# Last tiles' norm and stores rebuilt, step-size block in two products for three, and GpSimd's loads for the down sums begun behind their stores

## The reference

```python
h = rms_norm(x, norm_mix_pre)
proj = h @ w_in                      # q, k, v, z, xbc, and 32 columns of raw step sizes (dt_raw)
attn = neighbourhood_attention(q, k, v, rpb); attn = rms_norm(attn, attn_out_norm)
ssd = ssd_mixer(z, xbc, dt_raw, ...)  # dt = softplus(dt_raw + dt_bias), scans both ways
x = x + rms_norm(concat([attn, ssd]) @ w_out, norm_mix_post)
h = rms_norm(x, norm_ffn_pre)
gate = depthwise_conv(h @ w_gate, ffn_conv_w, ffn_conv_b)
f = (gelu(gate) * (h @ w_up)) @ w_down          # 2816 hidden channels
y = x + rms_norm(f, norm_ffn_post)
rms_norm(x, g) = x / sqrt(mean(x * x) + 1e-6) * g
```

## Time and profile before

| | |
|---|---|
| three runs | 2920.98 us median (2919.64 to 2925.11) |
| the profiled execution | 2929.13 us, span 2927.4 us |
| PE busy | 2810.8 us, 96% |
| DVE, ACT, POOL busy | 2036.0, 1279.8, 639.4 us |
| mean granted TensorE clock | 0.986 |

### The profile page before, as it was taken

One profiled execution on the slowest core, in us unless ns is written; L12 is line 12 of the kernel. 1 busy time (PEld: TensorE's weight loads), 2 busy tenths in 40 slices (PEclk: granted clock), 3 DMA queues, 4 the chain that ended last, 5 costly groups with the idle time before them and its releaser, 6 DMA issues.

```text
span 2927.4 us, 36565 instructions
## 1 busy us (share of the span) xinstructions
PE 2810.8 (96%) x12784; PEld 2227.4 (76%) x12784; DVE 2036.0 (70%) x3119; ACT 1279.8 (44%) x2547; POOL 639.4 (22%) x849
## 2 busy tenths in 40 slices
PE   7999999889999999999999999998999999999996
PEld 5878787568777778888778787875677788888885
DVE  3657754894788887775647577459857877777656
ACT  4224555345743223345533255552557333333443
POOL 4622222670014530000100322227500000000001
PEclk9999999989999999999999999999899999999998
DMA  7551232314535441253532422331246222114334
GB/s 224 140 146 55 67 102 90 113 31 157 182 130 194 166 165 51 69 175 115 193 102 69 130 61 73 120 119 51 80 140 197 77 80 78 67 58 155 97 115 140
DMA packets 150229, 334.84 MB, mean 114 GB/s; under 512 B 22353, under 2 KB 25073, under 8 KB 150048
## 3 DMA queue, kind: packets, MB, share of 16 engines
q1 hardware_dynamic: 112688, 202.54, 21.9%
q0 software_dynamic: 37360, 129.97, 13.3%
HBM read 264.51 MB, written 69.90 MB: 114 GB/s over the span
## 4 chain that ended last, share of the span: by engine, by line
PE 74%; DVE 15%; issue 4%; ACT 4%; DMA 2%; POOL 0%; SPq 0%; DVEq 0%; ACTq 0%; POOLq 0%
PE G L649 4%; PE G L651 4%; PE G L650 4%; PE A L1139 4%; PE A L1140 4%; PE A L1141 4%; PE A L1087 4%; PE A L1088 4%; PE A L1089 4%; PE G L1087 4%; PE G L1089 4%; PE G L1088 4%; PE G L679 3%; PE G L680 2%; PE G L681 2%
## 5 line engine op out<-in xcount | busy, mean ns | idle before, releaser
L1725 DVE TENSOR_TENSOR wlo<-raw,whi 128x512 fp32r<-128x512 f32 x630 | 437.4, 700 | 485.1 <-ACT whi L1212 482.6
L1212 ACT CAST whi<-raw 128x512 fp32r<-128x512 f32 x630 | 382.8, 619 | 447.2 <-PE A L1141 149.8
L649 PE MATMUL G<-arena_rounded,whi 128*128 128x512 f32 x800 | 330.6, 413 | 6.6 <-DVE wlo L1725 3.8
L651 PE MATMUL G<-arena_rounded,wlo 128*128 128x512 f32 x800 | 316.2, 395 | 0.0
L650 PE MATMUL G<-arena_rounded,whi 128*128 128x512 f32 x800 | 316.1, 395 | 0.0
L1087 PE MATMUL G<-arena_rounded,whi 128*128 128x512 f32 x560 | 222.3, 397 | 3.1 <-DVE wlo L1725 1.5
L1087 PE MATMUL A<-arena_rounded,whi 128*128 128x512 f32 x560 | 222.0, 396 | 2.7 <-DVE small L2315 1.6
L1089 PE MATMUL G<-arena_rounded,wlo 128*128 128x512 f32 x560 | 221.5, 396 | 0.0
L1089 PE MATMUL A<-arena_rounded,wlo 128*128 128x512 f32 x560 | 221.5, 396 | 0.0
L1088 PE MATMUL G<-arena_rounded,whi 128*128 128x512 f32 x560 | 221.5, 395 | 0.0
L1088 PE MATMUL A<-arena_rounded,whi 128*128 128x512 f32 x560 | 221.4, 395 | 0.0
(11 more groups left out here) (345 smaller groups left out, 6222.4 us busy)
## 6 DMA issues: line engine op xcount, KB each, us to landing
raw<-w_gu_tiles SPq DMA_DIRECT2D x184, 256.0 KB, 3.3
raw<-w_out_rows SPq DMA_DIRECT2D x144, 256.0 KB, 2.9
raw<-w_tok_tiles SPq DMA_DIRECT2D x96, 256.0 KB, 2.7
raw<-w_in_tiles SPq DMA_DIRECT2D x92, 256.0 KB, 2.9
raw<-sums_of_down SPq DMA_DIRECT2D x88, 256.0 KB, 2.7
raw<-w_down_rows SPq DMA_DIRECT2D x66, 256.0 KB, 2.8
f_by_chunk<-small POOLq DMA_DIRECT2D x24, 512.0 KB, 4.6
arena<-w_down_rows POOLq DMA_DIRECT2D x22, 512.0 KB, 7.2
```

What stands on the lines that cost most here:

```text
L649: nc.tensor.matmul(out, whi[:, u % SPLIT_SLOTS, w], hi, start=first, stop=False)
L651: return nc.tensor.matmul(out, wlo[:, u % SPLIT_SLOTS, w], hi, start=False, stop=last)
L1212: nc.scalar.copy(whi[:, u % SPLIT_SLOTS, w], weights_of(u)).then_inc(S["hi_split"], 1)
L1725: tt(wlo[:, u % SPLIT_SLOTS, w], weights_of(u), whi[:, u % SPLIT_SLOTS, w].bitcast(F), ALU.subtract).then_inc(S["lo_split"], 1)
```

## The change

Four things are edited.

1. The step-size block. DVE writes the low part of the 32 real columns into the zero columns 32 to 63 of `whi`, so that two products for three (`gemm_dt`) give high and low halves in different partitions of the same bank. ACT copies partitions 32 to 63 out, and DVE adds them. `tail_stats` and `tail_out` of the previous sequence's last four tiles move one input block ahead, to blocks 1 and 2.
2. GpSimd's loads for the down sums: those of block p are issued right behind the stores of sums p - 1, before the wait for the next f.
3. The last four tiles. In sequence 1 SP loads x1 of tiles 4 to 7 into four buffers of their own during down, at n = 37, 41, 45 and 57, behind the waits that the next sequence's x has in sequence 0. ACT squares channels 512 to 1023 at n = 68 to 71, DVE multiplies them by the gain at n = 69 to 72. After the last product ACT squares the other half and takes the root, GpSimd multiplies that half by the gain, and DVE makes one instruction of the rest (`last_out`). SP stores.
4. Tile 4's `last_out` stands before the last bank's `add_down`.

```diff
+DT_UNITS = range(UNITS_TO[DT_BLOCK + 2], UNITS_TO[DT_BLOCK + 3])
+DT_ROWS = 32
...
+X1_EARLY = (0, 1, 4, 2)
+LAST_SQUARED, LAST_GAINED = (68, 69, 70, 71), (69, 70, 71, 72)
...
+                    elif n in X_LOADED and X_LOADED.index(n) in X1_EARLY:
+                        at_x = X_LOADED.index(n)
+                        i_x1 = 4 + X1_EARLY.index(at_x)
+                        sp.wait_ge(S["weights_used"], nth("weights_used", UNITS_TO[J_DOWN + (3 if at_x in (0, 1, 4) else 5)]))
+                        sp.wait_ge(S["x1_saved"], nth("x1_saved", 16 * TT))
+                        sp.dma_start(x_tile(at_x), x1_dram[i_x1 * P:(i_x1 + 1) * P, :].rearrange("p (a n) -> p a n", a=2)).then_inc(S[f"x_in{at_x}"], 16)
                     load(J_DOWN + o, slice(i, i + 1))
+                if s == SEQS - 1:
+                    for i in range(4, TT):
+                        sp.wait_ge(S["yo_ready"], nth("yo_ready", i + 1))
+                        sp.dma_start(y[s, i * P:(i + 1) * P, :].rearrange("p (a n) -> p a n", a=2), x_tile(X1_EARLY[i - 4])).then_inc(S["last_saved"], 16)
...
+                def gemm_dt(b, banks):
+
+                    for j, u in enumerate(DT_UNITS):
+                        pe.wait_ge(S["lo_split"], nth("lo_split", u + 1))
+                        for kk in range(UC):
+                            w = whi[:, u % SPLIT_SLOTS, kk * P:(kk + 1) * P]
+                            for h in range(2):
+                                k = j * UC + kk
+                                nc.tensor.matmul(G[:, banks[h], :], w, h_hi(k, h), start=k == 0, stop=False)
+                                m = nc.tensor.matmul(G[:, banks[h], :], w, h_lo(k, h), start=False, stop=k == KD - 1)
+                        m.then_inc(S["weights_used"], 1)
...
-                    if s and b in (2, 3):
-                        tail_stats(s - 1, 2 * b)
-                        tail_stats(s - 1, 2 * b + 1)
+                    if s and b in (1, 2):
+                        tail_stats(s - 1, 2 * b + 2)
+                        tail_stats(s - 1, 2 * b + 3)
                     if b == DT_BLOCK:
                         act.wait_ge(S["y_saved"], nth("y_saved", 0))
+                        nc.scalar.copy(u_, psum(b)[DT_ROWS:2 * DT_ROWS])
                         nc.scalar.activation(x_, psum(b)[0:32], ACT.Identity, bias=prm[0:32, PC["dt_bias"]:PC["dt_bias"] + 1]).then_inc(S["in_copied"], 1)
...
+                    if s == SEQS - 1 and n in LAST_SQUARED:
+                        i = 4 + LAST_SQUARED.index(n)
+                        act.wait_ge(S["d_added"], nth("d_added", 4 + i - 4 + 1))
+                        nc.scalar.activation(unused[:, HALF:T], o_row(i)[:, HALF:T], ACT.Square, accum_out=stat[:, 2, i:i + 1]).then_inc(S["half_squared"], 1)
...
                 split_to(uend(j_in(DT_BLOCK)) + 1)
                 dve.wait_ge(S["in_copied"], nth("in_copied", DT_BLOCK + 1))
+                after(tt(x_, x_, u_, ALU.add))
                 stt(u_, x_, -1.0, x_, ALU.mult, ALU.max).then_inc(S["exp_dt"], 1)
...
+                def last_out(i):
+
+                    dve.wait_ge(S["yo_rt"], nth("yo_rt", i + 1))
+                    at = inverse(stat[:, 3, i:i + 1])
+                    at_x = X1_EARLY[i - 4]
+                    dve.wait_ge(S["gained"], i - 3)
+                    dve.wait_ge(S[f"x_in{at_x}"], 16 * (SEQS + 1))
+                    stt(x_tile(at_x), gained(i), at, x_tile(at_x), ALU.mult, ALU.add).then_inc(S["yo_ready"], 1)
...
                     pool.dma_start(f_dram[p], f_home(p)).then_inc(S[f"f_moved{p % 2}"], 16)
-                    if s == 0 and p:
-                        sums_of_down(p - 1)
+                    if s == 0:
+                        if p:
+                            sums_of_down(p - 1)
+                        if p < HALF_K:
+                            load_for_sums(p)
...
                 if s == SEQS - 1:
-                    pool.wait_ge(S["y_saved"], nth("y_saved", 16 * TT))
+                    for i in range(4, TT):
+                        pool.wait_ge(S["d_added"], nth("d_added", 9 + i - 4))
+                        nc.gpsimd.tensor_tensor(gained(i)[:, 0, :], o_row(i)[:, 0:HALF], gain_ffn[:, 0:HALF], ALU.mult).then_inc(S["gained"], 1)
```

More of the change, by code:

```diff
@@ L478, in x_tile, with gained @@
             return arena.views[2][:, k0 - 16:k0 - 14, :].rearrange("p a n -> p (a n)")[:, HALF:HALF + T].rearrange("p (a n) -> p a n", a=2)
+        def gained(i):
+            return x_tile((3, 5, 6, 7)[i - 4])
         def x1_ring(i):
@@ L537, in encoder @@
             table_saved fixed_made fixed_saved x_in0 x_in1 x_in2 x_in3 x_in4 x_in5 x_in6
-            x_in7 act_step x_res3 x1_in0 x1_in1 x1_in2 sw_in sw_saved"""
+            x_in7 act_step x_res3 x1_in0 x1_in1 x1_in2 sw_in sw_saved
+            half_squared half_gained gained last_saved"""
         S = {n: sem(n) for n in names.split()}
@@ L720, in _ @@
                     pe.wait_ge(S["in_copied"], nth("in_copied", b - 1))
-                    gemm(j_in(b), both(b), h_hi, h_lo)
+                    if b == DT_BLOCK:
+                        gemm_dt(b, both(b))
+                    else:
+                        gemm(j_in(b), both(b), h_hi, h_lo)
                 def in_g(i):
@@ L1307, in _ @@
                 act.wait_ge(S["cs_ready"], nth("cs_ready", 1))
[L1308 removed]
+                nc.scalar.copy(parts[0:32, :], x_).then_inc(S["parts_hi"], 1)
                 split_to(UNITS_TO[J_V] + 10)
                 act.wait_ge(S["q_rows"], nth("q_rows", 1))
[L1311 removed]
+                nc.scalar.copy(parts[64:96, :], q_).then_inc(S["parts_hi"], 1)
                 split_to(UNITS_TO[J_X] + 2)
@@ L1724, in split_to @@
                         w = slice(0, UNIT_CHUNKS[u] * P)
-                        tt(wlo[:, u % SPLIT_SLOTS, w], weights_of(u), whi[:, u % SPLIT_SLOTS, w].bitcast(F),
-                           ALU.subtract).then_inc(S["lo_split"], 1)
+                        if u in DT_UNITS:
+                            first, source = (a.rearrange("p (k n) -> p k n", k=UC) for a in (whi[:, u % SPLIT_SLOTS, :], weights_of(u)))
+                            tt(first[:, :, DT_ROWS:2 * DT_ROWS], source[:, :, 0:DT_ROWS], first[:, :, 0:DT_ROWS].bitcast(F),
+                               ALU.subtract).then_inc(S["lo_split"], 1)
+                        else:
+                            tt(wlo[:, u % SPLIT_SLOTS, w], weights_of(u), whi[:, u % SPLIT_SLOTS, w].bitcast(F),
+                               ALU.subtract).then_inc(S["lo_split"], 1)
                         units[0] += 1
@@ L2366, in _ @@
                         tail_out(s, TAILS_AT.index((o, i - 1)))
+                    if s == SEQS - 1 and n in LAST_GAINED:
+                        i = 4 + LAST_GAINED.index(n)
+                        dve.wait_ge(S["half_squared"], i - 3)
+                        ts(stat[:, 0, i:i + 1], stat[:, 2, i:i + 1], 1.0 / D, EPS, ALU.mult, ALU.add)
+                        tt(gained(i)[:, 1, :], o_row(i)[:, HALF:T], gain_ffn[:, HALF:T], ALU.mult).then_inc(S["half_gained"], 1)
                     if s + 1 < SEQS and n in (X_SQUARED[3] + 1, 7 * HALF_K - 1):
                         front_scale(s + 1, int(n == 7 * HALF_K - 1))
-                for b in range(4):
-                    add_down(6, b)
-                if s == SEQS - 1:
-                    for i in range(4, TT):
-                        tail_out(s, i)
+                def last_out(i):
[5 more added lines that the diff above has]
+                    stt(x_tile(at_x), gained(i), at, x_tile(at_x), ALU.mult, ALU.add).then_inc(S["yo_ready"], 1)
+                if s + 1 < SEQS:
+                    for b in range(4):
+                        add_down(6, b)
+                else:
+                    for b in range(3):
+                        add_down(6, b)
+                    last_out(4)
+                    add_down(6, 3)
+                    for i in range(5, TT):
+                        last_out(i)
         @block.gpsimd
@@ L2651, in _, with at_sums, load_for_sums @@
                 nc.gpsimd.memset(t(2, 1, 1025), 0.0).then_inc(S["pads"], 1)
-                def sums_of_down(i):
-                    first, second = arena[:, K + 2 * (i % 2), :], arena[:, K + 2 * (i % 2) + 1, :]
-                    a11, a21, a12, a22 = first[:, 0:HALF], first[:, HALF:T], second[:, 0:HALF], second[:, HALF:T]
+                def at_sums(i):
+                    return arena[:, K + 2 * (i % 2), :], arena[:, K + 2 * (i % 2) + 1, :]
+                def load_for_sums(i):
+                    first, second = at_sums(i)
                     if i >= 2:
@@ L2659, in sums_of_down @@
                     pool.dma_start(second, w_down[K2[i]]).then_inc(S["sw_in"], 16)
+                def sums_of_down(i):
+                    first, second = at_sums(i)
+                    a11, a21, a12, a22 = first[:, 0:HALF], first[:, HALF:T], second[:, 0:HALF], second[:, HALF:T]
                     pool.wait_ge(S["sw_in"], 32 * (i + 1))
@@ L2698, in _ @@
```

(17 more changed lines are left out.)

20 lines of the change are left out of this document (11 added, 9 removed).

## The result

| | before | after |
|---|---|---|
| first comparison, median | 2921.48 us (10 runs) | 2913.95 us (10 runs), ratio 0.9965, 95% interval 0.9952 to 0.9977 |
| second comparison, median | 2922.75 us (11 runs) | 2909.83 us (5 runs), ratio 0.9953, 95% interval 0.9940 to 0.9965 |
| first profiled execution | 2929.13 us | 2917.64 us, span 2915.9 us |

The account below looks back on a forecast made before the run. TensorE, busy 96% of the span, was taken as the bound. Terms 7.4 + 8.0 + 6.3 − 1.2 = 20.5 us took the profiled 2929.13 to 2908.6 and 2920.98 to 2900.5, range 2895 to 2909.

Parts of the forecast that it names:

- so 2.1 of extra DVE time fits there: Periods of seven, sequence 0: the additions' 2.1 us a period on DVE fits before TensorE takes the next unit.
- x1 in SP's queue: Sequence 1's down: early x1 loads delay weights near n = 57, 1.2 us lost, bounds 0 and 3.2.
- The step-size block, −7.4: Input blocks: 16 matmuls fewer a sequence at 0.231 us, 3.7 us each, 7.4 gained in all.
- two splits with a slack of 0.3: DVE's splits behind the step-size block: both still ready for TensorE, with 0.3 and 0.3 to 0.5 us to spare.
- rival 2: Step-size block gains nothing, as two splits come late and push the chain after them: 2908 us, chance 0.06.
- I see nothing that uncovers it: Tail work one input block ahead: 5.0 us of DVE stays hidden under a block's 11.2 us of matmuls.
- GpSimd's loads, −8.0: Seven of sequence 0: moved loads bring nearly sequence 1's time, 8.0 us gained, bounds 8.9 and nothing.
- the lead of 3.2: Seven of sequence 1: DVE's split of the next block's second unit ends 3.2 us before TensorE takes it.
- Rival 1: Seven, sequence 0: GpSimd's additions cost as much in the new place, 8.8 us, the 8.0 vanishes: 2908.5, chance 0.15.
- the bound of 3.2: x1 loads in sequence 1's down: at worst they lose 3.2 us, all that sequence 0 loses in its x burst.
- The end, −6.3: Behind TensorE's last matmul: rebuilt last tiles end at 2921.15 us, 6.3 gained, bounds 8.0 and 3.3.
- None of the terms is in that difference: Sum: the profiled execution lies 8 us above the three runs' median, and no term is part of that.

Follow-up runs that it names:

- experiment 2: Kernel before with the step-size block in two products and the tails of sequence 0 one block ahead: 2918.45 against 2924.85 us, ratio 0.9972.
- experiment 1: Kernel before with only the step-size block in two products, tails left in blocks 2 and 3: 2928.23 against 2923.83 us, ratio 1.0016.
- experiment 8: Changed kernel with x1 of tile 7 at n = 61 and GpSimd's additions left out, so its down product is wrong: 2903.47 us, ratio 0.9925.
- experiment 9: Changed kernel with x1 of tile 7 at n = 61 and GpSimd's additions waiting for DVE's first three sums: 2910.95 us, ratio 0.9954.
- Experiments 5 to 7: x1 of tile 7 at n = 61, 0.9953; wait at n = 57 without its load, 0.9931; next sequence's x later too, 0.9931.
- experiment 3: Kernel before with only GpSimd's loads for the down sums moved behind their stores: 2918.02 us, ratio 0.9981.
- experiment 5: Changed kernel with x1 of tile 7 loaded at n = 61 instead of 57: 2909.34 us, ratio 0.9953 to the kernel before.
- experiment 7: Changed kernel with x1 of tile 7 at n = 61 and the next sequence's x at n = 60, 62, 64, 67, 70: 2905.04 us, ratio 0.9931.

## Why the prediction was wrong

The direction and the ranking of the mechanisms held; two terms of the sum were mis-sized, and something outside the sum was left out. The terms were 4.5 us too high by their own sizes and 5.8 by the rest of the profiles, the stretches that no term spoke of took 3 more, and the measured time lies above the range.

The steps that failed are "so 2.1 of extra DVE time fits there" (3.25 us a period, not 2.1) and the price of 1.2 for x1 in SP's queue (3.2).

- **The step-size block, −7.4.** Right: 3.4 between 33 and 174 us in the first profile, 3.7 in the input blocks of sequence 1 (133.4 to 129.7), and 6 to 8 us in experiment 2. (The mean of 4.4 above holds 0.7 of half-clock matmuls near that sequence's start, in three of four profiles of before and one of four of after.) The two splits with a slack of 0.3 held, rival 2 did not come true. But "I see nothing that uncovers it", said of the tails' work, priced the moved work and missed what the move is for. ACT's wait for the landed y stands ahead of the evacuation, and experiment 1 shows 4.3 us of stalls, with 2.1 at half the clock behind them, when it isn't moved. The copy to `u_` stands behind that wait in the code, and the prediction did not follow it.
- **GpSimd's loads, −8.0.** Mis-sized: −5.5. The step that failed is "so 2.1 of extra DVE time fits there". The stretch in the new place is not 2.1 a period but 3.25 (32.5 us in ten). Two neighbouring sums take 1.1 and 1.0 more, and two splits before them 0.5 and 1.1. With it the lead of 3.2 is used up: the split at 966.82 ends at 967.50, where PE would have taken the unit at 967.45. The 2.1 was the figure of the old place, where only some instructions with two SBUF inputs met the additions. Rival 1 named the right place and mechanism and was too dear at its price: 3.0 us are left to be had, not 8.8 (experiment 8).

  By the Trainium skill, SBUF — State Buffer, "Who interferes with whom", a DVE instruction with two SBUF inputs meets GpSimd's reads, and one with at most one doesn't, outside the modes that take both port pairs. The trace agrees on who: in experiment 9, 0.68 with a PSUM input (987.41) and 1.41 for a split 1.3 us earlier, both under the additions. A `TENSOR_SCALAR` at 989.13, one tensor and a column of scalars, grew from 0.81 to 1.78; no row tells in which mode it ran. Of a full block the trace shows less: an addition takes 1.6 and the sum beside it grows by 1.1.
- **x1 in SP's queue, +1.2.** Mis-sized: the stalls add up to 2.8 to 3.6 in the four profiles, and the whole of down grew by 3.2 to 3.8, at and above the bound of 3.2. The prediction took the first stall of the earlier trace rows and left the two behind it to the x loads that follow. Sequence 1 has one load there, and all three stalls. That one late tile uses up the queue's lead for the units behind it is a reading; the rows show one long wait and two short ones in a row. Experiments 5 to 7 show what makes it late: a wait for TensorE set where SP runs ahead by four units, and a transfer behind it that passes before the weights.
- **The end, −6.3.** Right in sum (6.3), in part by luck, as terms were off and cancelled. Two `last_out` were stretched to 2.32, by 2.1 together where 0.9 was counted, and DVE was done 8.0 behind the last matmul's start for 7.2. The last store took 3.7 for 3.9, and from its landing to the end it was 5.1 for 5.7. Half squares and gains cost nothing.
- **The median.** "None of the terms is in that difference": the profile of before lay 8 us above the runs, and the forecast took the whole 20.5 from the lower number. Three later profiles of the same kernel have spans of 2922.7, 2920.9 and 2919.6. In the rest all four lie within 5.3 us, so the 14.7 isn't a matter of which profile was taken; the open stretches were no part of the sum.

By the sizes measured the sum is 7.4 + 5.5 + 6.3 − 3.2 = 16.0, against 14.7 in the rest of four profiles each. Most of the difference is the 1.2 lost in the output product of sequence 0, a stall that no term spoke of and whose cause stays open.

## What to carry to other kernels

A load put into the queue that feeds the bottleneck costs its wait first and its bytes second. Set it where the wait is already met when the queue comes there: three or four steps, about the depth of the raw buffers, made 3 us in each sequence here. When a phase is shortened, look for what the waits behind it allow to be late, not only at the instructions that fit beneath: the same edit was 0.2% slower or 0.3% faster, and most of that went by where the previous stores were issued. GpSimd's additions were paid by DVE here, by its instructions with two SBUF inputs above all; moving the additions moved the bill, and only leaving them out showed the floor.

## What the runs showed of the hardware

**Stretched beside GpSimd.** Under GpSimd's additions (4 in 6.4 us) DVE's 128x512 with two SBUF inputs went from 0.69 to 1.66 and 1.78, a `TENSOR_SCALAR` of 128x1024 from 0.81 to 1.78, and one with a PSUM input stayed at 0.68.

**Half the clock behind a stall.** Windows of experiment 1: ahead of its stall, the stall, behind it, and after.

```profile
1519.33:1535.15 15.82, 15.59 (x67) 12.28 (x66) 5.86 (x7) 5.80 (x11) 2.98 (x8) 1.00 0.53 179
1535.15:1539.30 4.15, 0.40 (x2) 0.00 (x0) 3.03 (x3) 2.91 (x3) 0.00 (x0) 0.81 0.00 0
1539.40:1544.50 5.10, 5.10 (x12) 4.04 (x13) 4.61 (x4) 1.39 (x3) 0.00 (x0) 0.50 0.16 51
1544.60:1560.00 15.40, 15.40 (x68) 12.41 (x67) 15.05 (x15) 3.37 (x5) 0.00 (x0) 1.00 0.24 69
```

After 3.95 us without a matmul the granted clock is 0.50, the 1.2 GHz level: twelve matmuls at 0.43 for 0.23, 2.1 us on top of the stall itself. Stalls of 2.1 to 3.0 us in the output product had 1.4 us of it behind them in four profiles; one of 2.2 had none.

**A stretch that varies by itself.** One of the open stretches in four kernels: sequence 0 of the first profile of before and of experiment 3, sequence 1 of the changed kernel and of experiment 5.

```profile
179.46:743.19 563.73, 537.01 (x2634) 419.18 (x2634) 381.80 (x682) 276.31 (x667) 192.90 (x239) 0.97 0.30 95
```

```profile
179.93:738.94 559.01, 529.94 (x2635) 414.59 (x2635) 380.71 (x682) 276.01 (x668) 195.43 (x239) 0.99 0.31 96
```

```profile
1616.35:2182.58 566.23, 537.11 (x2635) 419.82 (x2635) 381.19 (x682) 275.89 (x667) 194.31 (x239) 0.98 0.30 95
```

```profile
1611.70:2178.34 566.64, 536.15 (x2635) 418.39 (x2635) 382.22 (x682) 276.11 (x667) 193.61 (x239) 0.98 0.30 95
```

The same work takes 559 to 567 us. DVE, ACT and GpSimd are busy alike; it is PE, with many short idle times in the scan, that gets a granted clock between 0.97 and 0.99. In one 20 us window of experiment 7 it was 0.65, in the neighbouring place of the second profile of the changed kernel 0.85. Such differences are of the size of the scatter of 5 to 10 us between runs; that they make it is not shown, as most runs have no profile. Why the windows with the new block have the longer values more often stays open, as does a stall in the output product of sequence 0, 1.0 to 3.0 us in twelve profiles with the block and 0.4 to 1.2 in six without.
